# Hybrid retention and attention block on one core: second plain bank's seed one piece up in VectorE's order, all squares of the x rows on ScalarE, x forms 3 and 4 moved up in the lead-in, and the odd retention head's projection taken out of its banks sooner

## What is computed

```python
h = rms_norm(x, norm1_g)
rq, rk, rv, rg, aq, ak, av = split(h @ w_in)                    # 8 heads of 128 each
ret = silu(rg) * head_group_norm(retention(rotary(rq), rotary(rk), rv))
att = chunk_attention(rms_norm(aq), rms_norm(ak), av, rel_bias) # softmax over a band of chunks
x = x + concat(ret, att) @ w_out
h = rms_norm(x, norm2_g)
x = x + square(relu(h @ w_ff1)) @ w_ff2                         # 2048 -> 8192 -> 2048
```

## Time and profile before

| | |
|---|---|
| median of 3 runs | 1118.41 us |
| the profiled execution | 1118.55 us |
| its span, first to last instruction | 1116.8 us |
| TensorE busy | 1102.4 us (99%) |
| VectorE, ScalarE, GpSimd busy | 884.1, 689.7, 54.0 us |
| mean granted TensorE clock | 1.00 |
| TensorE's share of the chain that ended last | 90% |

### The profile page before, as it was taken

The page is one execution under the profiler, slowest core; times in us unless marked ns, Lnnn a source line. Parts: engine busy times, 40 slices in busy tenths (PEclk is TensorE's granted clock), DMA queues, the critical chain, the costliest instruction groups (busy, mean ns, idle before and its releaser), DMA issues.

```text
span 1116.8 us, 13188 instructions
## 1 busy us (share of the span) xinstructions
PE 1102.4 (99%) x5198; PEld 931.8 (83%) x5198; DVE 884.1 (79%) x881; ACT 689.7 (62%) x809; POOL 54.0 (5%) x66
## 2 busy tenths in 40 slices
PE   9899999999999999999999999999999999999998
PEld 8779979979978888888888888888888888888887
DVE  7968868877878768879788779788779787879784
ACT  6764665655565446667755577755577655577652
POOL 0100100100100000000000000000000000000000
PEclk9999999999999999999999999999999999999999
DMA  9975675575686466787797787797787788787782
GB/s 362 283 253 171 180 244 190 177 245 179 182 257 225 170 226 192 263 265 229 245 277 233 259 274 225 248 270 238 257 278 221 249 275 233 257 283 214 246 275 97
DMA packets 42958, 263.81 MB, mean 236 GB/s; under 512 B 4752, under 2 KB 6544, under 8 KB 15120
## 3 DMA queue, kind: packets, MB, share of 16 engines
q1 hardware_dynamic: 36704, 220.22, 53.0%
q0 software_dynamic: 5760, 41.95, 20.4%
q10 hardware_dynamic: 432, 0.81, 0.2%
HBM read 260.85 MB, written 2.10 MB: 235 GB/s over the span
## 4 chain that ended last, share of the span: by engine, by line
PE 90%; DVE 4%; ACT 2%; DMA 2%; issue 1%; POOL 0%; ACTq 0%; DVEq 0%
PE acc L871 10%; PE acc L867 10%; PE acc L869 10%; PE acc L739 6%; PE acc L746 6%; PE acc L752 6%; PE bankC L829 4%; PE acc L829 4%; PE acc L824 4%; PE bankC L822 4%; PE bankC L824 4%; PE acc L822 4%; DVE w_lo L1404 2%; PE acc L591 2%; PE acc L596 2%; PE acc L603 2%
## 5 line engine op out<-in xcount | busy, mean ns | idle before, releaser
L1690 DVE TENSOR_TENSOR w_lo<-raw,w_hi 128x2048 fp32r<-128x2048 f32 x180 | 410.9, 2289 | 126.8 <-ACT w_hi L1207 126.5
L1207 ACT ACTIVATE w_hi<-raw 128x2048 fp32r<-128x2048 f32 x180 | 344.8, 1917 | 219.0 <-PE acc L871 144.5
L1404 DVE TENSOR_TENSOR w_lo<-raw,w_hi 128x1024 fp32r<-128x1024 f32 (+1 forms) x152 | 165.9, 1105 | 37.1 <-ACT w_hi L993 37.1
L993 ACT ACTIVATE w_hi<-raw 128x1024 fp32r<-128x1024 f32 (+1 forms) x152 | 142.2, 964 | 25.0 <-DVE raw L1413 15.4
L739 PE MATMUL acc<-w_hi,hT_hi 128*128 128x384 f32 (+1 forms) x416 | 107.5, 375 | 4.0 <-DVE acc L1426 2.2
L867 PE MATMUL acc<-w_hi,hF_hi 128*128 128x512 f32 x256 | 100.8, 394 | 0.0
L871 PE MATMUL acc<-w_hi,hF_lo 128*128 128x512 f32 x256 | 99.7, 390 | 0.0
L752 PE MATMUL acc<-w_lo,hT_hi 128*128 128x384 f32 (+1 forms) x416 | 99.1, 356 | 0.6 <-DVE w_lo L1404 0.6
L869 PE MATMUL acc<-w_lo,hF_hi 128*128 128x512 f32 x256 | 99.6, 389 | 0.0
L746 PE MATMUL acc<-w_hi,hT_lo 128*128 128x384 f32 (+1 forms) x416 | 99.5, 357 | 0.0
L867 PE MATMUL acc<-w_hi,dF_hi 128*128 128x512 f32 x248 | 96.8, 390 | 0.0
(11 more groups left out here) (262 smaller groups left out, 1810.0 us busy)
## 6 DMA issues: line engine op xcount, KB each, us to landing
raw<-in_w_up SPq DMA_DIRECT2D x64, 1024.0 KB, 6.1
raw<-in_w_down SPq DMA_DIRECT2D x64, 1024.0 KB, 5.8
raw<-in_w_ret SPq DMA_DIRECT2D x32, 1024.0 KB, 5.2
raw<-in_w_att SPq DMA_DIRECT2D x28, 768.0 KB, 4.2
raw<-in_w_out SPq DMA_DIRECT2D x16, 1024.0 KB, 4.8
raw<-in_w_up POOLq DMA_DIRECT2D x16, 1024.0 KB, 9.0
raw<-in_w_down POOLq DMA_DIRECT2D x16, 1024.0 KB, 9.0
raw<-in_w_ret POOLq DMA_DIRECT2D x8, 1024.0 KB, 9.2
```

What stands on the lines that cost most here:

```text
L993: nc.scalar.activation(piece(w_hi, q, 0, n), raw[:, r, half * n:(half + 1) * n], ACT.Copy).then_inc(hi_done, 1)
L1207: nc.scalar.activation(w_hi[:, ring(s)], raw[:, r, :], ACT.Copy).then_inc(slab_hi, 1)
L1404: nc.vector.tensor_tensor(piece(w_lo, q, 0, n), raw[:, IN_PLAN[i, READ_AT.get(step, step)][0], half * n:(half + 1) * n], piece(w_hi, q, 0, ...
L1690: nc.vector.tensor_tensor(w_lo[:, ring(s)], raw[:, r, :], w_hi[:, ring(s)].bitcast(f32), ALU.subtract).then_inc(slab_lo, 1)
```

## The change

- `set_w` goes from position 24 to 23 in VectorE's table, in every block.
- `x_squares` does all eight squares of x on ScalarE; `x_mean_squares` on VectorE keeps the sum and the added EPS, and waits for the eight.
- `s_third` goes from position 8 to 7, ahead of `x_mean_squares`.
- On ScalarE `ret_proj(u+1)` stands ahead of `ret_scale(u)`, and waits for the even head's last matmul from `rp` and for its gate, which are the readers of `rp`.

```diff
             def ret_proj(u):
                 i, step = u // 2, "HZ"[u % 2 == 0] + "2"
+                if u % 2:
+                    act.wait_ge(r_y, u)
+                    act.wait_ge(r_gate_ok, u)
                 evacuate(4 * i + 3 + u % 2, in_first(i, step) + 1, (bH, bY) if u % 2 else (bZ, bW), rp, N_RET)
...
                 for c in range(OUT_GROUPS):
                     act.wait_ge(x_in[c], 16)
-                    squares(0, c, ss, c)
+                    for m in range(MT):
+                        squares(m, c, ss, MT * c + m)
...
+                at_piece(i + 1, 0, ret_proj, u + 1)
                 at_piece(i + 1, 0, ret_scale, u)
-                at_piece(i + 1, 0, ret_proj, u + 1)
...
             def x_mean_squares():
-                for c in range(OUT_GROUPS):
-                    dve.wait_ge(x_in[c], 16)
-
-                    cols = xs[:, 1, c * N:(c + 1) * N]
-                    nc.vector.tensor_tensor_reduce(rp[:, c % MT, :], cols, cols, 1.0 / D_MODEL, 0.0,
-                                                   ALU.mult, ALU.add, ss[:, 1, c:c + 1]).then_inc(squared_dve, 1)
-                    if c:
-                        dve.wait_ge(squared_dve, c)
-                dve.wait_ge(squared_dve, OUT_GROUPS)
-                dve.wait_ge(squared, OUT_GROUPS)
+                dve.wait_ge(squared, MT * OUT_GROUPS)
...
-            at_piece(0, PIECES - 1, x_mean_squares)
-            at_piece(0, 8, s_third)
+            at_piece(0, 7, s_third)
+            at_piece(0, 7, x_mean_squares)
...
-                at_piece(i, 24, set_w, i)
+                at_piece(i, 23, set_w, i)
```

More of the change, by code:

```diff
@@ L201, in hybrid_block @@
         squared = sem("squared")
-        squared_dve = sem("squared_dve")
         ms_ok = sem("ms_ok")
@@ L1240, in stream_squares @@
                 for m in range(MT):
-                    squares(m, c, ss2, OUT_GROUPS + MT * c + m, hid[:, 0, :])
+                    squares(m, c, ss2, MT * OUT_GROUPS + MT * c + m, hid[:, 0, :])
             group(G_OUT + 1, N, N, {2: [x_forms_first, lambda: stream_squares(0)]})
@@ L1758, in stream_mean_squares @@
             def stream_mean_squares():
-                dve.wait_ge(squared, OUT_GROUPS + MT * OUT_GROUPS)
+                dve.wait_ge(squared, 2 * MT * OUT_GROUPS)
                 nc.vector.tensor_reduce(ms2[:], ss2[:], AX.X, ALU.add).then_inc(ms2_ok, 1)
```

## The result

Five runs of the changed kernel had a median of **1112.87 us** (1112.82 to 1112.96), five of the kernel before beside them 1118.52 (1118.36 to 1118.54): 5.65 us less, a ratio of 0.995 with a 95% interval of 0.9936 to 0.9963. The profiled execution took 1112.92 us (before 1118.55) and its span is 1111.1 us (before 1116.8).

The account below looks back on a forecast made before the run. TensorE bounds the kernel, busy 1102.4 of 1116.8 us, so only its late starts, some 14 us, can be won. -4.56 - 1.19 + 0.32 = -5.43 us from 1118.41 gives 1113.0 us, range 1111.8 to 1116.0.

Parts of the forecast that it names:

- The seed: In each block: set_w ahead of piece 26's subtraction ends 1.14 us sooner; 4.56 us gained over four blocks.
- The odd head: At the output projection's start: ScalarE copies the odd head's projection before scaling, so r_qk's transposes lose their stall; 1.19 us gained.
- The lead-in: Around Q1, up to piece 12: four more squares on ScalarE, mostly covered by two waits for weights; +0.32 us net.
- the rule of the Trainium skill: Four added squares: multiplications belong on VectorE, not ScalarE; by price alone they cost 0.56 us, giving 1113.2 us.
- The moved mixes: Behind Q1: s_third's mixes run earlier, so piece 11's subtraction is held only by ScalarE's copy; no size of its own.
- A second leg (1): In the blocks: TensorE's restart or GpSimd's power holds a_qk's transposes, 0.55 us a block; 1115.3 us, chance 0.08.
- Uncovered squares (2): Before Q1: all 3.14 us of added ScalarE squares go through and stay; 1115.8 us, chance 0.08.
- the lighter VectorE pays (3): Before the first block's Z1: relieving VectorE of squares gains 0.8 us instead of a loss; 1111.8 us, chance 0.06.
- A late load (5): In the blocks: weights asked for 1.14 us sooner arrive late, so the blocks give nothing; 1117.5 us, chance 0.04.
- The fall of the clock (4): Ahead of Q1: TensorE's longer idle time drops its clock to 1.2 GHz for 15 us; 1123.6 us, chance 0.04.

Follow-up runs that it names:

- the squares alone: The kernel before with all eight squares on ScalarE, but s_third left between VectorE's subtractions of pieces 10 and 11: 1118.88 us against 1118.50.
- the seed alone: The kernel before with only set_w moved from position 24 to 23 on VectorE: 1113.94 us against 1118.39.
- two more squares: The changed kernel with the last column group's two squares done a second time on ScalarE, same result: 1114.22 us.
- the lead-in's part alone: The kernel before with only all eight squares on ScalarE and s_third ahead of x_mean_squares: 1118.51 us, ratio 1.0002.

## Why the prediction was right

It said 1113.0 us, and 1112.87 came; what made it right was following the chain of waits link by link. That the sum came within 0.1 is luck in part: two of its three terms were 0.1 to 0.35 us off, in opposite directions.

- **The seed** was to give 1.14 a block, 4.56 in all. The block's step fell by 85.31 - 84.17 = 1.14, and T3 of the kernel with this part alone by 4.54. The links came one by one as worked out: the seed is there before TensorE asks, piece 27 comes 150.01 - 147.24 = 2.77 behind Z1's first matmul (2.72 and a few hundredths foretold), the transposes 6.29 (6.3 foretold). The stall for a_qk stayed, as said: 0.46 in the row, and by starts 153.53 - (151.99 + 0.91) = 0.63, where 0.7 was foretold. The sum didn't depend on its length, since the place of the transposes came from ScalarE's line.
- **The odd head** was to give 1.19. Alone it moved R by 1.19, of which 0.08 had come by T3 and isn't its own, so it gave 1.11 there and 0.98 in the medians. Inside the whole change R moved 5.62, of which 4.51 had come by T3, so 1.11 again. The missing 0.08 is the distance of the two pairs of transposes, 0.22 where the prediction had worked out 0.14.
- **The lead-in** is the term that was mis-sized: +0.32, measured +0.12 in the medians and -0.03 at T0. The mechanism held (3 us of squares, nearly all inside two waits for loads), but I took the larger of the squares' steps, 0.82, for all of them, while they alternate and average 0.78, and counted 0.14 of the fourth square's wait for its rows as absorbed, where all 0.23 were. The copies of pieces 10 and 11 came 1.07 later instead of 1.3, and the second wait of 0.90 with its 0.09 step took that nearly whole: 32.42 instead of the 32.7 foretold. Z1 of block 0 came 0.06 later and not 0.3. By the 0.56 us that the prediction worked out from the rule of the Trainium skill (ScalarE: Activation LUTs, Rules for kernel authors), the miss would have been larger. The prediction set ScalarE's step of 0.82 against VectorE's busy time of 0.68, which are two measures: from start to start VectorE's squares took 0.61 to 0.62 (25.55, 26.16, 26.78, 27.39 in the kernel before). So a square is indeed dearer on ScalarE, 0.78 against 0.61, and more so than the prediction had it, and it costs nothing as long as it fills a wait. Past that, the two further squares cost all of their 1.3 us.
- **The moved mixes** were named as what lets TensorE catch up behind Q1, and the squares alone show it: without them the first head's transposes come 0.32 later behind Q1, and T0 is 0.31 later.
- **The rivals.** A second leg (1) would have left the blocks at 0.55 each; they gave 1.14. Uncovered squares (2) would show in T0; they don't. That the lighter VectorE pays (3) fell too: it waits for ScalarE longer than before (0.78 at 33.28, before 0.58). A late load (5) would have shown as a wait of ScalarE in the blocks; the seed alone gave all it promised. The fall of the clock (4) didn't come in any of the five runs of the changed kernel, with 1.13 us idle ahead of Q1. The prediction called 0.9 the longest pause so far, which was a misreading: TensorE already sat idle for 1.08 us at the start of the projection (its matmul at 7.53 in the kernel before) and for 1.56 at the start of the program, at a granted clock of 1.00. Only the pause of 2.5 with two more squares was longer, and its profiled execution has 1.00 too. Elsewhere the rival isn't wholly gone. Of the 51 runs of kernels with eight or more squares on ScalarE, three have a mean granted clock under 1.00: one with the lead-in's part alone (0.951, 1119.52 us against a median of 1118.51) and two with two more squares (0.998, 1114.22 and 1114.49). Of 78 runs without these squares none has. No trace of the three was kept, so where their clock fell stays open; the first took 1.0 us more, and without the three the medians would be 1118.51 (unchanged) and 1114.20.

What stays open: whether the 0.34 us between the sum of the parts and the whole is scatter or a small gain of the parts together. The traces speak for scatter: after and the seed alone agree within 0.03 us at T3, and in the profiled executions the parts give 4.59 + 1.22 + 0.04 = 5.85 us, more than the 5.63 of the whole.

## What to carry over

When several small stalls follow each other, look for the one line of work that feeds them all and for an instruction in it that the line doesn't need; moving that gave more (1.14) than the first stall showed (0.55). Put additional work on an engine where its trace shows a wait for a load, and count up to the cover's end, since the first four squares (3.1 us) were free here and the next two were paid in full (1.3 us, beside 0.21 that weights landing earlier hid). Two fixes for one stall don't add, and moving the consumer up an in-order queue delays what is next in that queue.

## What the hardware did unasked

GpSimd's small power operations take 0.72 us (128x2) and 1.03 us (128x4) when VectorE has no subtraction under way as they start, but longer beside one that it has begun before: 1.55 for 128x2, and for 128x4 2.10 beside a subtraction of 1.23 (at 38.20 in the kernel after) and 1.67 beside one of 0.95 (at 122.44). The Trainium skill (SBUF — State Buffer, SBUF: two separate sides) describes a port pair shared by the two as an exclusive lock that whichever starts first holds for its whole instruction. The row at 30.03 agrees: it starts 0.24 behind the first of the two subtractions that begin at 29.79 and last 2.35 together, and ends at 31.58, some 0.6 behind the end of that first one. In the other direction the trace doesn't show it: after `a_rs` had begun (149.30 to 150.33 in the kernel after), the subtraction at 149.99 took its usual 1.23 us. The measurement decides: here only the small operation of GpSimd pays, by 0.6 to 1.1 us, and it matters where ScalarE or VectorE waits for its result.

TensorE's idle time of 2.5 us in the lead-in left the granted clock at 1.00 in the profiled execution, in a stretch with several other stalls; two other runs of that kernel show a mean of 0.998.
